# Down projection of a gated MLP in seven block products, taken in five stages of gate tiles

## The chip, the cores and the metric

One core of a Trainium2 chip runs the whole layer in one launch. The metric is the device time of that launch in microseconds (us). The kernel before takes 1263.61 us, the median of three runs (1263.59 to 1263.95).

## The reference

The layer takes 512 tokens of one group and 256 of another (768 in all), D_MODEL 1024. A token mixer comes first; the change doesn't touch it. What matters is the second sub-layer, a gated MLP with 2816 hidden channels (22 tiles of 128):

```python
def conv_ffn(hn, w_ffn_in, conv_w, conv_b, w_ffn_down):
    u, v = jnp.split(hn @ w_ffn_in, 2, axis=-1)
    up = jnp.pad(u, ((0, 0), (1, 1), (0, 0)))
    uc = conv_b
    for t in range(3):
        uc = uc + up[:, t:t + L] * conv_w[t]
    return (jax.nn.gelu(uc) * v) @ w_ffn_down

h = h + conv_ffn(rmsnorm(h, norm_ffn), ...)
return rmsnorm(h, norm_final)
```

Everything is float32. The down projection is a (768 x 2816) by (2816 x 1024) product.

## The kernel before

A float32 product is made of three TensorE passes: each operand is split into a high part (a rounded copy, ScalarE, `hi_...`) and a low part (the difference to it, VectorE, `lo_...`), and high x high, high x low and low x high are accumulated in PSUM. Weights come by DMA into two buffers (`raw`, `raw2`), and their two parts go into a ring of 8 places of 512 columns (`ring`). `PLACE` and `ORD` give each piece its place and its number; ScalarE and VectorE fill the ring some 5 or 6 places ahead of TensorE, in an order written out by hand (`hi_upto`, `lo_upto`), and semaphores (`flo`: low part written, `fdone`: product done) tie the engines.

The input projection already runs in seven block products for eight. Per pair i (one tile of u, one of v) there are seven products A11, A12, S2, S1, S3, A22, S4 of 4 x 3 matmuls with 384 token columns (line 1669). The weight blocks for S1, S2, S3 and A22 are differences, made by GpSimd (`combine`, lines 1362 to 1373). ScalarE and VectorE join the products (`first_copy`, `second_copy`, `third_copy`, `join_...`), then comes the convolution (`centre`, `conv`, line 1241), the GELU (line 730), the product with v (`gate`, line 1253) and the split of the result into `g` (`gate_hi` line 737, `gate_lo` line 1257).

The order is cut into three chunks, of 8, 8 and 6 pairs (`CHUNKS`). After the pairs of a chunk its part of the down projection runs (`down`, line 1730): for either half of the 1024 output columns, unit by unit of 256 channels, six token tiles of 128 x three passes, each a matmul of a 128x128 gate tile (stationary) with 512 weight columns (moving). Each token tile has a PSUM bank for a half; VectorE adds the finished bank to the stream `h` (`residual`, line 1137). In the last chunk the second half is taken token tile by token tile, so that the closing norm of one tile (square on ScalarE line 798, mean, root, scale, store) runs beside the matmuls of the next. The down weights are plain: one DMA of 512 KB per unit (line 393), one ScalarE copy (line 659) and one VectorE difference (line 1155) of 1024 columns, nothing for GpSimd.

At the end of a chunk A22 of the last pair waits for the copy of S3 out of its bank, since no other product can be put between:

```python
            def pair_end(i):
                pe.wait_ge(p13_cp, i + 1)
                product(i, A22, BANK_A[i % 2], False)
```

Of the kernel before, what the change touches and what calls it, by code (L numbers as in the profile page):

```python
# [30 lines left out]
ALU = mybir.AluOpType  # L31
ACT = mybir.ActivationFunctionType
F32 = mybir.dt.float32
# [21 lines left out]
CHUNKS = ((0, 8), (8, 16), (16, 22))  # L55
# [8 lines left out]
UNITS = U_D + NF  # L64
# [20 lines left out]
ORD, PLACE, UPLACE, FREED, PIECES = {}, {}, {}, {}, {}  # L85
# [3 lines left out]
for _lo, _hi in CHUNKS:  # L89
    for _f in taken(_lo, _hi):  # L90
        ORD[_f], PLACE[_f], PIECES[_p], FREED[_p] = len(ORD), _p, _f, (True, len(ORD) + 1)
        _p += 1
    for _n in range(U_D + _lo, U_D + _hi):
        UPLACE[_n] = _p
        PIECES[_p], PIECES[_p + 1] = None, _n
        FREED[_p] = FREED[_p + 1] = (False, _n + 1)
        _p += 2
# [4 lines left out]
def raw_of(i):  # L102

    return (i + (i >= CHUNKS[0][1])) % 2


def loads_of(i):
    return sum(raw_of(j) == raw_of(i) for j in range(i + 1))


REGION = 4 * (NT * D + 2 * 8 * T + 3072 + 4 * T + HALF + 14 * HK * HALF)
# [56 lines left out]
def build(nc, x_s, x_p, units, pairs, vec, w_final, ident_d, masks_d, rot_d, strips_d, y_s, y_p):  # L168
    with ExitStack() as ctx:
# [6 lines left out]
        def region(*tensors):  # L176
# [36 lines left out]
        _, g, raw2, tb, u2, v2, cb, mid, af = region(  # L213
            ("b0", [P, NT, D], F32), ("g", [P, 2, 8, T], F32R), ("raw2", [P, 2, UNIT], F32), ("tb", [P, 2, PIECE], F32),
            ("u2", [P, 2, T], F32), ("v2", [P, T], F32), ("cb", [P, T], F32), ("mid", [P, HALF], F32),
            ("af", [P, 7, 2, HK, HALF], F32R))
        *_, wfin, junk2, hw = region(
            ("c0", [P, NT * D + 2 * 8 * T + 3072 + 4 * T + HALF], F32), ("wfin", [P, D], F32), ("junk2", [P, PIECE], F32), ("hw", [P, NT, D], F32))

        _, sums0 = region(  # L220
            ("e0", [P, NT * D + 2 * 8 * T + 3072 + 4 * T + HALF], F32), ("sums0", [P, 7, 2, HK, HALF], F32))
# [28 lines left out]
        pu_ld = [sem("pair_u_loaded0"), sem("pair_u_loaded1")]  # L250
        pv_ld = [sem("pair_v_loaded0"), sem("pair_v_loaded1")]
# [4 lines left out]
        dn, out_rdy, out_rdy0 = sem("down_done"), sem("out_ready"), sem("out_first_half_ready")  # L256
        half_sq, half_var, root_done, weighed = sem("half_squares"), sem("half_variance"), sem("root_inverted"), sem("out_weighed")

        raws = (raw, raw2)

        def source(i, x):

            r = raws[raw_of(i)]
            if i == 0 and x in FIRST:
                return FIRST[x]
            return {A11: r[:, 0, 0:PIECE], A12: r[:, 0, PIECE:UNIT], S4: r[:, 1, PIECE:UNIT], S3: r[:, 1, 0:PIECE],
                    S1: tb[:, 0, :], S2: tb[:, 1, :], A22: tb[:, 1, :]}[x]
# [16 lines left out]
        BANK_A, BANK_C = (0, 6), 7  # L284

# [42 lines left out]
        def _(sp):  # L328
# [47 lines left out]
            for lo, hi in CHUNKS:
                for i in range(lo, hi):
                    if i == 1:

                        sp.wait_ge(w_done, 2 * NT)  # L380
                        sp.dma_start(raw2[:, 0, :], pairs[i, 0]).then_inc(pu_ld[1], 16)
                        sp.dma_start(raw2[:, 1, :], pairs[i, 1]).then_inc(pv_ld[1], 16)
                    elif i == 0 or i == lo + 1:
                        load_pair(i, None, U_D + lo - 1)
                    else:
                        load_pair(i, i - 2, None)
                last_raw = hi - 1 if raw_of(hi - 1) == 0 else hi - 2
# [19 lines left out]
        def _(act):  # L407
# [235 lines left out]
            def hi_piece(i, x):  # L643
                if x in (A11, A12):
                    act.wait_ge(pu_ld[raw_of(i)], 16 * loads_of(i))
                elif x == S4:
                    act.wait_ge(pv_ld[raw_of(i)], 16 * loads_of(i))
                else:
                    act.wait_ge(t_done, 4 * i + ((S1, S2, S3, A22) if i == 1 else (S1, S3, S2, A22)).index(x) + 1)
# [3 lines left out]

            def hi_unit(n):
                act.wait_ge(raw_ld[n % 2], 8 * (n - n % 2) + 16)
                p = UPLACE[n]
                await_place(act, p)
                await_place(act, p + 1)
                act.activation(ring[:, p % 8:p % 8 + 2, 0, :], pieces(raw[:, n % 2, :]), ACT.Copy).then_inc(hi_split, 1)
# [3 lines left out]
            def hi_upto(p):  # L663
                for q in range(hi_next[0], min(p, PLACES - 1) + 1):
                    if isinstance(PIECES[q], tuple):
                        hi_piece(*PIECES[q])
                    elif PIECES[q] is not None:
                        hi_unit(PIECES[q])
# [47 lines left out]
            def centre(i):  # L716
# [3 lines left out]
                if i >= 1:  # L720
                    act.wait_ge(g_lo, i)
# [10 lines left out]
            def gate_hi(i, lo):  # L732
                act.wait_ge(g32_done, i + 1)
                if lo > 0:

                    act.wait_ge(unit_done, U_D + lo)
                act.activation(g[:, 0, i - lo, :], cb[:], ACT.Copy).then_inc(g_hi, 1)
# [24 lines left out]
            for lo, hi in CHUNKS:  # L762
                for i in range(lo, hi):
# [18 lines left out]
                    if i > lo:  # L782
                        gate_hi(i - 1, lo)
                hi_upto(PLACE[hi - 1, A22] + 6)
                centre(hi - 1)
                gelu(hi - 1)
                gate_hi(hi - 1, lo)
                for n in range(U_D + lo, U_D + hi):
                    hi_upto(UPLACE[n] + 6)
            for t in range(NT):  # L790
                act.wait_ge(h_up, (1 + 2 * len(CHUNKS)) * NT - NT + t + 1)
                act.wait_ge(fdone, len(ORD))
                act.drain()
                act.activation(junk2[:], h[:, t, 0:PIECE], ACT.Square, accum_out=stat[:, 4, t:t + 1]).then_inc(half_sq, 1)
            for t in range(NT):
                act.wait_ge(h_up, (2 + 2 * len(CHUNKS)) * NT - NT + t + 1)
                act.drain()
                act.activation(junk2[:], h[:, t, PIECE:D], ACT.Square, accum_out=stat[:, 0, t:t + 1]).then_inc(sq_done, 1)
                act.wait_ge(var_done, 2 * NT + t + 1)
                act.activation(stat[:, 2, t:t + 1], stat[:, 1, t:t + 1], ACT.Sqrt).then_inc(sd_done, 1)  # L800
                act.wait_ge(root_done, t + 1)
                act.wait_ge(weighed, t + 1)
                act.activation(hw[:, t, 0:PIECE], hw[:, t, 0:PIECE], ACT.Copy, scale=stat[:, 3, t:t + 1]).then_inc(out_rdy0, 1)
# [3 lines left out]
        def _(dve):  # L807
# [344 lines left out]
            def lo_unit(n):  # L1152
                dve.wait_ge(hi_split, n + 1)
                p = UPLACE[n] % 8
                dve.tensor_tensor(ring[:, p:p + 2, 1, :], pieces(raw[:, n % 2, :]), ring[:, p:p + 2, 0, :].bitcast(F32),
                                  ALU.subtract).then_inc(lo_split, 1)

            def combine_second(x):

                r = raws[raw_of(1)]  # L1160
                b11, b12, b22 = r[:, 0, 0:PIECE], r[:, 1, 0:PIECE], r[:, 1, PIECE:UNIT]
                if x == S1:
                    dve.wait_ge(pu_ld[raw_of(1)], 16)
                    dve.wait_ge(pv_ld[raw_of(1)], 16)
                    dve.wait_ge(t_done, 4)
                    ins = dve.tensor_tensor(tb[:, 0, :], b12, b11, ALU.subtract)
                elif x == S3:
                    ins = dve.tensor_tensor(b12, b22, b12, ALU.subtract)
                else:
                    dve.wait_ge(t_done, 5)  # L1170
                    ins = dve.tensor_tensor(tb[:, 1, :], b22, tb[:, 0, :], ALU.subtract)
                ins.then_inc(t_done, 1)

            lo_next = [BASE]

            def lo_upto(p):
                for q in range(lo_next[0], min(p, PLACES - 1) + 1):
                    what = PIECES[q]
                    if isinstance(what, tuple):
                        i, x = what  # L1180
                        lo_piece(i, x)
                    elif what is not None:
                        lo_unit(what)
# [65 lines left out]
            def gate(i):  # L1249
                dve.wait_ge(gelu_done, i + 1)  # L1250
                dve.wait_ge(c12_dn, i + 1)
                dve.wait_ge(c22_dn, i + 1)
# [600 lines left out]
```

## Time and profile before

| | |
|---|---|
| median of 3 runs | 1263.61 us |
| profiled execution, its own time | 1264.54 us |
| span of its trace | 1262.7 us |
| TensorE (PE) busy | 1232.3 us, 98% |
| VectorE (DVE) busy | 711.9 us, 56% |
| ScalarE (ACT) busy | 490.9 us, 39% |
| GpSimd (POOL) busy | 128.9 us, 10% |
| down projection, matmuls | 792 |
| input projection of the MLP, matmuls | 1848 |

Times in the trace are counted from the start of the span. The duration of a matmul there contains its way through the pipeline, so the rate is to be read from a run of matmuls, not from one. Idle time stands in square brackets, with what ended it. The MLP runs from 738 us to the end.

### The profile page before, as it was taken

The page shows a single profiled execution, that of the slowest core. Times are in us where ns is not written, and L with a number is a line of the kernel's source. Part 1 is how long each engine was busy: PE and PEld are TensorE (multiplying, and loading weights), DVE is VectorE, ACT ScalarE, POOL GpSimd, SP SyncE. Part 2 cuts the span into 40 slices and gives each one's busy share as a digit, 9 for nine tenths or more (in the row PEclk, how much of TensorE's full clock was granted, in tenths as well). Part 3 has the DMA queues.
Part 4 walks back from the last instruction along what each step waited for, and adds up shares of the span by engine and source line. Part 5 has one row for each costly group of instructions (what it writes and reads, how often), then busy time and mean ns, then how long its engine had stood idle before and what let it go on. Part 6 is the DMA issues. An engine that isn't in the chain of part 4 may idle for free.

```text
span 1262.7 us, 18036 instructions
## 1 busy us (share of the span) xinstructions
PE 1232.3 (98%) x7088; PEld 1120.7 (89%) x7088; DVE 711.9 (56%) x969; ACT 490.9 (39%) x724; POOL 128.9 (10%) x93
## 2 busy tenths in 40 slices
PE   6999999999999999999999988999999999999998
PEld 5999899989998998888888878998889998899986
DVE  7494586377368463223223698775237774337755
ACT  5353344245146152212221255554125653135534
POOL 0000000000000000000000303430124420124200
PEclk9999999999999999999999999999999999999999
DMA  4311111101121112121215102222201213112122
GB/s 171 136 35 51 63 51 51 62 33 50 34 78 36 46 37 68 67 67 50 76 56 184 34 34 86 82 68 78 89 34 67 67 42 121 72 34 81 53 84 100
DMA packets 23180, 86.10 MB, mean 68 GB/s; under 512 B 2512, under 2 KB 2768, under 8 KB 23120
## 3 DMA queue, kind: packets, MB, share of 16 engines
q1 hardware_dynamic: 22544, 83.90, 19.4%
q10 hardware_dynamic: 576, 1.38, 0.3%
q8 instruction: 41, 0.67, 0.2%
q14 instruction: 19, 0.16, 0.0%
HBM read 82.12 MB, written 3.15 MB: 68 GB/s over the span
## 4 chain that ended last, share of the span: by engine, by line
PE 92%; DVE 4%; DMA 1%; issue 1%; ACT 1%; DVEq 1%; SPq 0%; ACTq 0%
PE ps L1425 58%; PE ps L1669 23%; PE ps L1522 3%; PE ps L1462 3%; PE ps L1515 1%; PE ps L1532 1%; PE ps L1450 1%; DVE af L1196 1%; PE ps L1452 1%; DVE h L1137 1%; DMA raw<-in_units 1%; DVE ring L1150 1%; PE ps L1407 0%; PE ps L1498 0%; PE ps L1507 0%
## 5 line engine op out<-in xcount | busy, mean ns | idle before, releaser
L1425 PE MATMUL ps<-hn,ring 128*128 128x256 f32 (+1 forms) x2544 | 462.5, 337 | 0.3 <-DVE hn L839 0.3
L1425 PEld LDWEIGHTS ps<-hn,ring 128*128 128x128 f32 x2544 | 388.3, 191 | 46.7 <-issue 0.7
L1669 PE MATMUL ps<-af,ring 128*128 128x384 f32 x1848 | 325.7, 336 | 10.9 <-DVE af L1196 3.9
L1669 PEld LDWEIGHTS ps<-af,ring 128*128 128x128 f32 x1848 | 321.3, 189 | 15.0 <-DVE af L1196 4.8
L1425 PE MATMUL ps<-ring,g 128*128 128x512 f32 x792 | 180.9, 390 | 0.8 <-issue 0.8
L1425 PEld LDWEIGHTS ps<-ring,g 128*128 128x128 f32 x792 | 148.4, 188 | 32.6 <-issue 2.0
L810 DVE TENSOR_TENSOR ring<-raw,ring 128x1024 fp32r<-128x1024 f32 x68 | 83.1, 1224 | 119.2 <-ACT ring L415 114.8
L464 ACT ACTIVATE sig<-ps 128x768 f32<-128x768 f32 x36 | 29.2, 812 | 179.9 <-PE ps L1425 179.8
L1150 DVE TENSOR_TENSOR ring<-raw,ring 128x512 fp32r<-128x512 f32 x88 | 74.0, 877 | 15.9 <-ACT ring L652 15.7
L415 ACT ACTIVATE ring<-raw 128x1024 fp32r<-128x1024 f32 x68 | 71.7, 1055 | 28.8 <-PE ps L1425 10.2
L1384 POOL TENSOR_TENSOR sums<-raw 128x512 f32<-128x512 f32 x1 | 1.3, 1289 | 706.9 <-DMA raw<-in_pairs 706.9
L1425 PE MATMUL ps<-gated,ring 128*128 128x512 f32 (+1 forms) x384 | 68.2, 337 | 0.0
L1425 PE MATMUL ps<-ring,merged 128*128 128x512 f32 x288 | 66.9, 391 | 0.1
L1425 PEld LDWEIGHTS ps<-gated,ring 128*128 128x128 f32 x384 | 59.6, 190 | 7.8
L888 DVE TENSOR_TENSOR pt<-ps,strips 128x512 f32<-128x512 f32 (+1 forms) x48 | 28.5, 601 | 65.3 <-PE ps L1452 65.3
L1425 PEld LDWEIGHTS ps<-ring,merged 128*128 128x128 f32 x288 | 53.6, 188 | 11.5 <-issue 0.5
L652 ACT ACTIVATE ring<-raw 128x512 fp32r<-128x512 f32 x88 | 52.3, 624 | 29.1 <-PE ps L1425 29.1
L1137 DVE TENSOR_TENSOR h<-ps,h 128x512 f32<-128x512 f32 x48 | 32.8, 691 | 42.4 <-PE ps L1425 42.2
L477 ACT ACTIVATE yc<-tree_k 128x768 f32<-128x768 f32 x28 | 25.6, 916 | 76.5 <-DVE tree_k L975 41.5
L1150 DVE TENSOR_TENSOR ring<-tb,ring 128x512 fp32r<-128x512 f32 x63 | 43.5, 694 | 16.5 <-ACT ring L652 16.5
L1241 DVE SCALAR_TENSOR_TENSOR cb<-u,vecs,cb 128x511 f32<-128x511 f32 x88 | 51.1, 622 | 2.0 <-issue 0.4
L652 ACT ACTIVATE ring<-tb 128x512 fp32r<-128x512 f32 x63 | 37.1, 621 | 32.3 <-PEq L1763 14.1
(158 smaller groups left out, 1210.5 us busy)
## 6 DMA issues: line engine op xcount, KB each, us to landing
raw<-in_units SPq DMA_DIRECT2D x90, 512.0 KB, 3.5
raw<-in_pairs SPq DMA_DIRECT2D x44, 512.0 KB, 3.4
strips<-in_strips SPq DMA_DIRECT2D x4, 896.0 KB, 4.5
x_in<-in_x_s SPq DMA_DIRECT2D x4, 512.0 KB, 5.5
h<-in_x_s SPq DMA_DIRECT2D x1, 2048.0 KB, 8.4
y_s<-hw SPq DMA_DIRECT2D x4, 512.0 KB, 2.6
x_in<-in_x_p SPq DMA_DIRECT2D x2, 512.0 KB, 7.5
h<-in_x_p SPq DMA_DIRECT2D x1, 1024.0 KB, 10.5
```

The source lines that it names most:

```text
L415: act.activation(ring[:, 2 * slot:2 * slot + 2, 0, :], pieces(raw[:, slot % 2, :]), ACT.Copy).then_inc(hi_split, 1)
L464: ins = act.activation(sig[:, u % 2, :], dense(u), ACT.Sigmoid)
L652: act.activation(place_of(i, x, 0), source(i, x), ACT.Copy).then_inc(fhi, 1)
L810: dve.tensor_tensor(ring[:, 2 * slot:2 * slot + 2, 1, :], pieces(raw[:, slot % 2, :]), ring[:, 2 * slot:2 * slot + 2, 0, :].bitcast(F32), ...
L888: dve.tensor_tensor(pt[:, (i % 4) * NS:(i % 4) * NS + width], ps[:, 4 + i % 2, 0:width], strips[:, a, c0:c0 + width], ALU.mult).then_inc(r ...
L1137: return dve.tensor_tensor(hs, ps[:, bank, :], hs, ALU.add).then_inc(h_up, 1)
L1150: dve.tensor_tensor(place_of(i, x, 1), source(i, x), place_of(i, x, 0).bitcast(F32), ALU.subtract).then_inc(flo, 1)
L1241: ins = dve.scalar_tensor_tensor(out=cs, in0=u2[:, i % 2, c0 + frm:c0 + frm + w - 1], scalar=vecs[:, V_CONV + tap * NF + i:V_CONV + tap * ...
L1425: ins = pe.matmul(out, w if stationary_w else x, x if stationary_w else w, start=start and i == 0, stop=stop and i == 2)
L1462: ins = pe.matmul(ps[:, 6 + m // 4, col:col + 64], pt[:, (i % 4) * NS + c * P:(i % 4) * NS + (c + 1) * P], rv[:, m * P + 64 * a:m * P + 64 ...
L1522: ins = pe.matmul(out(c * P, P), yc[:, c * P:(c + 1) * P], facing(tree_q[:], what, c * P, P), start=True, stop=True)
L1669: ins = pe.matmul(ps[:, bank, 0:HALF], ring[:, p, a, k * P:(k + 1) * P], af[:, x, b, k, :], start=first and k == 0 and j == 0, stop=k == H ...
```

## The change

The down projection too is made of seven block products. The token tiles are halved (0 to 2, 3 to 5), the output columns are halved, and the inner dimension is halved inside each pair q of gate tiles (tiles 2q and 2q+1). Per pair q there are seven products of 3 token tiles x 3 passes, each matmul in the shape of before (128x128 gate form stationary, 512 weight columns moving). The code below is its core:

```diff
-CHUNKS = ((0, 8), (8, 16), (16, 22))
+STAGES = ((0, 5, (0, 1)), (5, 9, (2, 3)), (9, 13, (4, 5)), (13, 17, (6, 7)), (17, 22, (8, 9, 10)))
+DOWN = [(A11, A12, S2, S1, S3, S4, A22)] * 4 + [(A11, A12, S2, S1, S4, S3, A22)]
+DEST = {A11: (0, 0), A12: (0, 0), S2: (0, 1), S1: (1, 1), S3: (1, 1), S4: (0, 1), A22: (1, 0)}
+ON_A = (A11, S2, S3, A22)
+            def down(hi, qs, d):
+                for n, x in enumerate(order):
+                    steps = [(q, t) for t in range(3) for q in qs]
+                    for q, t in steps:
+                        if t == 0:
+                            pe.wait_ge(flo, ORD[down_pair(q), x] + 1)
+                            pe.wait_ge(g_lo, gate_form(q, x))
+                        if q == q0:
...
+                            elif x in (S2, S1, S3, S4, A22):
+                                before = {S2: A11, S1: A12, S3: S2, S4: S1, A22: S3}[x]
+                                pe.wait_ge(h_up, base + 3 * order.index(before) + t + 1)
+                        for j, (a, b) in enumerate(((0, 0), (0, 1), (1, 0))):
+                            ins = pe.matmul(ps[:, down_bank(hi, x, t), :], gate_place(q, x, b)[:, t * P:(t + 1) * P],
+                                            ring[:, p, a, :], start=q == q0 and j == 0 and x in (A11, A12, S1), ...)
```

Stage by stage: pairs 0 to 4 of the input projection, then q = 0, 1; pairs 5 to 8, then q = 2, 3; and so on; pairs 17 to 21, then q = 8, 9, 10. Partial sums of A11, S2, S3, A22 pile up in one set of banks, those of A12, S1, S4 in another, and after each product VectorE adds the three banks as they then stand to the quarter of `h` that `DEST` names (`down_sums`). The last product runs token tile by token tile into the closing norm; tiles 0 to 2 are finished after S4.

The down weights are loaded as pairs of half-columns, and are treated as the pairs of the input projection: seven pieces of 512 columns per q for ScalarE and VectorE, four differences of 512 columns for GpSimd. S1 is now written over the first raw block, so that it waits for the low part of A11:

```diff
+            if x == S1:
+                eng.wait_ge(pu_ld[raw_of(j)], 16 * loads_of(j))
+                eng.wait_ge(pv_ld[raw_of(j)], 16 * loads_of(j))
+                eng.wait_ge(flo, ORD[j, A11] + 1)
+                ins = eng.tensor_tensor(b11, b12, b11, ALU.subtract)
```

The gate tiles have forms too. The even tile gives A11 (its first 384 tokens) at once; with the odd tile VectorE makes four sums of 384 columns, and six forms are split:

```diff
             def gate(i):
+                if i % 2 == 0:
+                    dve.tensor_tensor(ge[:], cb[:], v2[:], ALU.mult).then_inc(g32_done, 1)
+                    return
                 dve.tensor_tensor(cb[:], cb[:], v2[:], ALU.mult).then_inc(g32_done, 1)
+                dve.tensor_tensor(GATE[S3], ge[:, 0:HALF], ge[:, HALF:T], ALU.subtract).then_inc(gs_done, 1)
...
+                dve.tensor_tensor(GATE[S2], GATE[A22], GATE[S3], ALU.subtract).then_inc(gs_done, 1)
+                dve.tensor_tensor(GATE[S1], ge[:, HALF:T], GATE[A22], ALU.add).then_inc(gs_done, 1)
+                if i == NF - 1:
+                    gate_lo(i - 1)
...
+                dve.tensor_tensor(GATE[S4], GATE[A12], GATE[S2], ALU.subtract).then_inc(gs_done, 1)
+            def gate_lo(i):
+                for x in GATES[:1] if i % 2 == 0 else GATES[1:]:
+                    dve.wait_ge(g_hi, gate_form(q, x))
+                    dve.tensor_tensor(gate_place(q, x, 1), GATE[x], gate_place(q, x, 0).bitcast(F32), ALU.subtract)
```

In the first four stages the forms of a q are finished one pair before the stage ends. In the last one q = 10 needs tiles 20 and 21; its raw weights (`raw3`) and its forms (`gf3`) lie in the memory of the token forms `af` of the input projection, so ScalarE's `gate_hi` for it waits for the last product of pair 21. The `pe.drain()` at the end of each half of a chunk is gone. The order of the work in the input projection is as before but for the stage borders.

## Rows read from the trace of the kernel before

**Rows 1.** The page, busy time of each engine over the span.
```profile
PE 1232.3 (98%) x7088; PEld 1120.7 (89%) x7088; DVE 711.9 (56%) x969; ACT 490.9 (39%) x724; POOL 128.9 (10%) x93
```

**Rows 2.** Chain that ended last from 1050 us: shares by line; pieces as start, us, what.
```profile
by line: PE ps L1425 52.3%; PE ps L1669 39.5%; DVE h L1137 1.9%; DMA raw<-in_units 1.7%; issue 1.1%; ACT junk L798 0.3%; ACT hw L803 0.3%; DVE ring L1150 0.3%; ACT v L714 0.2%; ACT mid L707 0.2%; DVE stat L1343 0.1%; ACT stat L800 0.1%; DVE
...
1052.18 32.68 PE ps L1425 x144
```

**Rows 3.** TensorE in order of time: start, us, instructions, idle before and its releaser.
```profile
1085.12 32.91 PE L1425 MATMUL ps<-ring,g 128*128 128x512 f32 x144 [0.26 <-issue]
1118.29 81.36 PE L1669 MATMUL ps<-af,ring 128*128 128x384 f32 x468 [0.26 <-DVE h L1137]
1199.83 2.36 PE L1669 MATMUL ps<-af,ring 128*128 128x384 f32 x12 [0.17 <-ACT mid L707]
1202.77 4.43 PE L1669 MATMUL ps<-af,ring 128*128 128x384 f32 x24 [0.58 <-ACT v L714]
1207.04 24.68 PE L1425 MATMUL ps<-ring,g 128*128 128x512 f32 x108
1231.98 24.75 PE L1425 MATMUL ps<-ring,g 128*128 128x512 f32 x108 [0.26 <-issue]
```

**Rows 4.** Busy time by stretch: window, its length, PE, PEld, DVE, ACT, POOL, clock, DMA.
```profile
867.80:934.08 66.28, 65.76 (x289) 53.83 (x289) 22.23 (x29) 11.41 (x15) 8.85 (x6) 1.00 0.20 70
934.08:1052.00 117.92, 117.12 (x672) 116.48 (x673) 81.01 (x120) 63.87 (x114) 37.27 (x26) 1.00 0.20 68
1052.02:1118.29 66.27, 65.75 (x290) 53.83 (x289) 22.77 (x29) 11.42 (x15) 8.88 (x6) 1.00 0.21 71
```

**Rows 5.** VectorE groups by shape from 740 us: count, busy us, mean ns, idle before.
```profile
L1150 DVE TENSOR_TENSOR ring<-tb,ring 128x512 fp32r<-128x512 f32 x63 | 43.5, 694 | 16.5 <-ACT ring L652 16.5
L1137 DVE TENSOR_TENSOR h<-ps,h 128x512 f32<-128x512 f32 x36 | 24.6, 692 | 34.0 <-PE ps L1425 33.9
L1257 DVE TENSOR_TENSOR g<-cb,g 128x768 fp32r<-128x768 f32 x22 | 21.1, 959 | 4.7 <-ACT g L737 2.7
L1233 DVE TENSOR_TENSOR v<-ps,v 128x384 f32<-128x384 f32 x22 | 12.3, 558 | 31.1 <-ACT v L714 31.1
```

**Rows 6.** VectorE in order of time, within two neighbouring pairs.
```profile
955.85 1.28 DVE L1150 TENSOR_TENSOR ring<-raw,ring 128x512 fp32r<-128x512 f32 x2
962.08 2.38 DVE L1150 TENSOR_TENSOR ring<-raw,ring 128x512 fp32r<-128x512 f32 x2
965.58 0.56 DVE L1221 TENSOR_TENSOR u<-ps,u 128x384 f32<-128x384 f32 x1 [1.12 <-PE ps L1669]
```

**Rows 7.** GpSimd in order of time, beside the second of these.
```profile
962.34 1.58 POOL L1362 TENSOR_TENSOR tb<-raw 128x512 f32<-128x512 f32 x1 [2.30 <-DVE ring L1150]
963.99 1.63 POOL L1365 TENSOR_TENSOR raw<-raw 128x512 f32<-128x512 f32 x1
```

**Rows 8.** VectorE from the last product of the last pair (TensorE 1207.2).
```profile
1207.71 2.36 DVE L1241 SCALAR_TENSOR_TENSOR cb<-u,vecs,cb 128x511 f32<-128x511 f32 x4
1210.98 0.96 DVE L1253 TENSOR_TENSOR cb<-cb,v 128x768 f32<-128x768 f32 x1 [0.91 <-ACT cb L730]
```

**Rows 9.** The start of the MLP: VectorE, then TensorE, in order of time.
```profile
763.91 3.47 DVE L1150 TENSOR_TENSOR ring<-raw,ring 128x512 fp32r<-128x512 f32 x2
769.45 3.20 DVE L1241 SCALAR_TENSOR_TENSOR cb<-u,vecs,cb 128x511 f32<-128x511 f32 x4
...
769.58 12.59 PE L1669 MATMUL ps<-af,ring 128*128 128x384 f32 x62 [2.88 <-DVE v L1227]
```

**Rows 10.** Busy time by stretch at the start of the MLP (columns as Rows 4).
```profile
760.00:770.00 10.00, 5.67 (x31) 5.03 (x30) 9.96 (x13) 5.81 (x11) 5.47 (x4) 1.00 0.13 50
770.00:780.00 10.00, 10.00 (x51) 10.00 (x50) 8.93 (x13) 6.26 (x11) 3.17 (x3) 0.83 0.31 107
```

**Rows 11.** The closing norm, VectorE and ScalarE in order of time.
```profile
1244.53 0.69 DVE L1137 TENSOR_TENSOR h<-ps,h 128x512 f32<-128x512 f32 x1 [1.37 <-PE ps L1425]
1246.75 0.49 DVE L1348 TENSOR_SCALAR hw<-hw,stat 128x512 f32<-128x512 f32 x1
1256.76 0.69 DVE L1137 TENSOR_TENSOR h<-ps,h 128x512 f32<-128x512 f32 x1 [1.15 <-PE ps L1425]
1258.98 0.72 ACT L803 ACTIVATE hw<-hw,stat 128x512 f32<-128x512 f32 x1 [0.23 <-DVE stat L1346]
```

**Rows 12.** DMA issues: source, KB each, median us from issue to landing.
```profile
raw<-in_pairs SPq DMA_DIRECT2D x44, 512.0 KB, 3.4
```

More of the change, by code:

```diff
@@ L795, in _ @@
[L795 to L799, printed above, removed]
+                if hi == NF:
+                    gate_hi(NF - 2)
+                    gate_hi(NF - 1)
+                for n, x in enumerate(DOWN[d]):
+                    hi_upto(PLACE[down_pair(qs[-1]), x] + 6)
+                    if n == 1 and hi < NF:
+                        gate_hi(hi - 1)
+                    if hi == NF and n == 2:
+                        act.wait_ge(fdone, ORD[NF - 1, S4] + 1)
+                        for t in range(3):
+                            act.wait_ge(h_up, down_base(d) + 3 + t + 1)
+                            squares(t, early(t), stat[:, 4, t:t + 1]).then_inc(half_sq, 1)
@@ new lines, in _ @@
+            base, order = down_base(len(STAGES) - 1), DOWN[-1]
+            for t in range(3):
+                act.wait_ge(h_up, base + 3 * order.index(S4) + t + 1)
+                squares(t, late(t), stat[:, 0, t:t + 1]).then_inc(sq_done, 1)
+            act.wait_ge(var_done, 2 * NT + 1)
+            act.activation(stat[:, 2, 0:3], stat[:, 1, 0:3], ACT.Sqrt).then_inc(sd_done, 1)
+            act.wait_ge(root_done, 1)
+            act.wait_ge(weighed, 3)
+            for t in range(3):
+                act.activation(hw[:, t, early(t)], hw[:, t, early(t)], ACT.Copy, scale=stat[:, 3, t:t + 1]).then_inc(out_rdy0, 1)
@@ L1249, in gate @@
             def gate(i):
+                q = i // 2
                 dve.wait_ge(gelu_done, i + 1)
@@ L1329, in _ @@
[L1329 to L1338 removed]
+                if hi == NF:
+                    gate(NF - 1)
+                    gate_lo(NF - 1)
@@ L1393, in _ @@
                 combine_tokens(pool, 0, x, s_done, 0)
-            combine(1, A22)
-            for i in range(2, NF):
-                for x in (S1, S3, S2, A22):
-                    combine(i, x)
+            pool.wait_ge(t_done, DIFF[1, S3])
+            for j, x in DIFFS[7:]:
+                difference(pool, j, x)
         @blk.tensor
@@ L1784, in _tables @@
+            for d, (lo, hi, qs) in enumerate(STAGES):
+                ffn(lo, hi, d)
+                down(hi, qs, d)
 def _tables():
@@ L1821, in _units @@
     out += [rows(w_out, k, half) for half in range(2) for k in range(KD // 2)]
-    for f0, f1 in CHUNKS:
-        out += [rows(w_ffn_down, k, half) for half in range(2) for k in range(f0 // 2, f1 // 2)]
     assert len(out) == UNITS
     pairs = [np.stack([cols(w_ffn_in, f * P), cols(w_ffn_in, FF + f * P)]) for f in range(NF)]
+    pairs += [np.stack([rows(w_ffn_down, q, 0), rows(w_ffn_down, q, 1)]) for q in range(NQ)]
     return np.stack(out), np.stack(pairs)
```

425 lines of the change are left out of this document (205 added, 220 removed).

## The prediction

> **What bounds the kernel now.** I read the page's busy shares first: TensorE is busy 98% of the span, and no other engine is over 56% [rows 1]. The chain of waits says the same for the part that the change touches: from 1050 us on 92% of it is TensorE's matmuls [rows 2]. So the time is the number of matmuls by their rate, plus the few gaps. The timeline of TensorE gives both: the three down parts are unbroken runs, the only gaps being 0.26 us after each drain, about 0.2 us once at a chunk's end, and 0.58 us where A22 of a chunk's last pair waits for the copy of S3 [rows 3]. The clock is at its upper level (2.4 GHz, granted 1.00) in these stretches [rows 4].
>
> **Matmuls removed.** Before there are 22 units x 2 x 6 tiles x 3 passes = 792, after 11 x 7 products x 3 tiles x 3 passes = 693. The shape stays, so the rate is the present one: 32.68 us / 144 = 0.227 us [rows 2]. After: 693 x 0.227 = 157.3 us. Before, the three down parts took 66.28 and 66.27 us [rows 4], and 1207.04 to 1256.73, 49.7 us [rows 3]: 182.2 us, drains and restarts included. Difference: **-24.9 us** (of it 22.5 by the count alone, the rest the five drains that go, each 0.26 us of idle and a pipeline run-out).
>
> **Two more stage ends.** The input projection keeps its 1848 matmuls. The wait for the copy of S3 now comes five times, not three: 0.58 us idle and some 0.16 us of run-out, twice: **+1.5 us** [rows 3].
>
> **VectorE in the down parts.** Here lies most of the work that is added. It was busy 22 of 66 us there [rows 4], a wide cover. Two pieces of 512 columns issue in 1.28 us [rows 6], and a sum out of PSUM takes 0.69 us [rows 5]. In a stage of two q a product lasts 18 x 0.227 = 4.09 us of TensorE; VectorE has 2 pieces (1.28), 3 sums (2.07) and a drain (0.1) in it: 3.45 us, 84%. Each product starts on banks whose sums of two products ago must be done, tile by tile, so VectorE may lag about one product. At a stage's start it does lag: in the pair before, the odd gate tile adds 4 sums and 6 low parts of 384 columns (0.47 us issue to issue, from the 0.56 us of a 384-column operation [rows 5]) for one low part of 768: (4 + 6) x 0.47 - 0.87 = +3.8 us. Following its order by hand, with the last convolution ending 4.6 us after the stage's last input product (2.9 us now [rows 8]), two pieces and the sums of A11 end at 7.9, gate and A12's sums at 12.2, S2's first sum at 14.7; S3 wants that one at 4 x 4.09 = 16.4 us. Slack 1.7 us. GpSimd's eight differences per stage eat some of it. In the trace two of them (1.58 and 1.63 us) made two pieces of VectorE take 2.38 us where they take 1.28 [rows 6, 7], and at 764 us two pieces took 3.47 us, at 769 us a convolution 3.20 for 2.36 [rows 8, 9]: 0.55 to 0.9 us lost per difference that overlaps. Two or three fall before S3. Bounds 0 and 2 us a stage; I take 0.3, as VectorE gains 0.6 us on TensorE in each product: **+1.2 us** for four stages. The Trainium skill ("SBUF — State Buffer", section "SBUF: two separate sides") has a rule that speaks against the change: a VectorE operation with both inputs in SBUF and a GpSimd operation exclude each other for the whole instruction. The rows above agree in kind, not in size: were each of three differences to cost a full 1.6 us, a stage would lose 3 x 1.6 - 1.7 = 3.1 us, four 12.4, and the sum below would be +2.2 us; I count that case in rival B. Sums out of PSUM have one input in SBUF and would be free by the rule.
>
> **VectorE in the input projection.** 81.0 us busy in 117.9 [rows 4], 10.0 us of 14.56 per pair. Two pairs gain 4 sums (1.9 us) and 7 low parts for 2 (+1.6): 23.5 us of 29.1. The odd one alone reaches 14 us, and the join after it, for which it now sits idle 1.12 us [rows 6], comes about 2 us late. Who waits: S1 of the next pair, two products (4.1 us) after it, for `join_last`. I take 0; bounds 0 and 0.5 us in each of ten odd pairs.
>
> **Weights.** The 22 unit loads become 22 half-pair loads of the same 512 KB; each lands in 3.4 us [rows 12]. At a down part's end the next pair's first load waits for the low part of A22 of q0, which is only two places ahead of it; 3.4 + copy 0.6 + low part 0.7 = 4.7 us against 4.1 us for two places. VectorE, blocked on it, loses about 1 us of a lead of 5 places (10 us). ScalarE was held longer by such a load at each of the present chunk ends, which cost TensorE 0.17 us [rows 3]. I take 0; the bound upwards is that VectorE's 1 us passes on to TensorE at each of nine borders.
>
> **The start of the last stage.** This is the one gap I expect plainly. TensorE takes the first tile of q 8, 9 and 10 at once, and for q 10 the A11 form of tile 20 must be ready after 6 x 0.227 = 1.36 us. Its low part is written by `gate_lo(20)`, which stands behind `gate(21)` and three sums in VectorE's queue, and that behind the last convolution and GELU. Now the gate product of the last pair starts at 1210.98, 3.8 us after the last input product [rows 8]. Then: 0.95 (product), 3 sums with one semaphore between (1.5), the low part (0.5), a semaphore: 6.8 us. Gap 6.8 - 1.4 = 5.4 us. Before, the gate tiles of the last pair were wanted only at the end of a half, so the same chain was hidden; that cover is gone. At the same time GpSimd makes the nine differences S1, S2, S3 of three q, 1.3 to 1.6 us each without a pause; four or five fall on this chain: 4.5 x 0.55 to 0.9 = 2.5 to 4 us. I take 3.0: **+8.4 us** (bounds 5.4 and 10).
>
> **The clock.** Before 770 us TensorE was busy 5.7 of 10 us, the last gap 2.88 us, and the granted clock then fell to 1.2 GHz for a while (mean 0.83 in the next 10 us) [rows 9, 10]; 62 matmuls of 384 columns took 12.59 us [rows 9], where at the rate of 468 in 81.36 us [rows 3] they take 10.8. A gap of over 5 us should do the same: **+1.8 us** (bounds 0 and 3.5).
>
> **The end.** The last product gives a token tile every 9 x 0.227 = 2.04 us, where now it is 4.09. The closing chain of one tile, from the sum (1244.53) to the end of the scaling (1247.24), is 2.71 us and had 1.37 us to spare [rows 11]. Now it is the slower one. Besides, VectorE comes late to it: in the last stage, from S1 on, it has the pieces, the sums, nine weighings and three scalings. By hand, from S2's end: sums of S1 end at 7.0, of S4 13.0, weighing and scaling of tiles 0 to 2 at 17.1, sums of S3 19.9 (TensorE 18.4), weighings 22.2; then three chains of 2.71 us, the third starting at 27.6, when TensorE ended at 24.7. From the last sum on the end is as now. **+3.0 us** (bounds 1.3, the chains alone, and 4.5).
>
> **Sum.** -24.9 + 1.5 + 1.2 + 8.4 + 1.8 + 3.0 = -9.0 us. The profiled execution took 1264.54 us, so 1255.5; it lies 0.9 us above the median of the runs, which gives **1254.6 us**.
>
> **Rivals.** *A, the gap is small:* GpSimd's differences are done early or don't meet the chain, and the clock holds: -24.9 + 1.5 + 5.4 + 3.0 = -15.0, 1248.6 us. For it: GpSimd is busy only 10% [rows 1]. Against: the nine differences start just there. *B, VectorE becomes the bound (slower):* if each of GpSimd's differences costs it 0.9 us, a product in a two-q stage needs 3.45 + 8 x 0.9 / 7 = 4.5 us, more than TensorE's 4.09; x 28 products = +11 us, and the odd pairs, at 14 us of 14.56, give 0.5 each, +5: -9.0 - 1.2 + 11 + 5 = +5.8, 1269.4 us. It decides from 0.56 us per difference on; the rows straddle that, but sums out of PSUM, 60% of the work, showed no stretching (692 ns mean [rows 5]), and VectorE's idle time takes up part. *C, between:* lateness in the stages of 1 us each, ten small waits in odd pairs (3 us): -9.0 + 2.8 + 3 = -3.2, 1260.4 us. *D, the weights come late:* 1 us at nine borders: 1263.6 us, no change. That the change doesn't remove the matmuls it says is excluded: they are counted in the loops.
>
> **How the numbers follow.** Forecast 0.50, A 0.20, C 0.16, D 0.05, B 0.09. The range leaves out B, D, and the lower part of A: 1249.5 to 1262 us. This kernel can be told from no change at about 0.2%, 2.5 us: faster 0.50 + 0.20 + 0.16 and a little of D, 0.88; within 0.2% 0.04; slower 0.08.
>
> **What would show it.** 693 matmuls in the down parts at 0.227 us each; a gap of 7 to 9 us on TensorE right after the first 6 of the last part, released by VectorE's low part of a gate form, and a granted clock under 1.00 behind it; five gaps of 0.6 us released by the copy of S3; VectorE busy 80 to 100% in the down parts, with pieces stretched and sums not; the last tiles' sums 2.7 us apart. The forecast is wrong if TensorE pauses inside the two-q parts (B, C), if the last gap is under 5 us (A), or if waits for DMA stand at the borders (D).

## The result, and the profile after

The changed kernel takes 1286.37 us, the median of four runs (1284.81 to 1288.06), against 1263.6 us before: ratio 1.018, interval 1.0163 to 1.0198. I had forecast 1254.6 us: the change costs 22.8 us where 9 were to be gained. The span of the profiled execution is 1283.9 us, 21.2 us more than before. The page after, busy shares (answers to [rows 1]):

```profile
PE 1222.6 (95%) x6989; PEld 1111.4 (87%) x6989; DVE 872.8 (68%) x1189; ACT 528.7 (41%) x832; POOL 195.7 (15%) x137
```

TensorE has its 99 matmuls less and is busy 9.7 us less, but it now stands idle. Where, its timeline shows (columns as [rows 3]; L1750 is the input projection, L1833 the down projection):

```profile
818.67 2.35 PE L1750 MATMUL ps<-af,ring 128*128 128x384 f32 x12 [0.58 <-ACT v L765]
826.28 3.71 PE L1750 MATMUL ps<-af,ring 128*128 128x384 f32 x12 [5.26 <-DVE v L1288]
829.83 28.76 PE L1833 MATMUL ps<-ring,gf 128*128 128x512 f32 x126
...
921.34 3.95 PE L1750 MATMUL ps<-af,ring 128*128 128x384 f32 x12 [5.26 <-DVE v L1288]
...
1014.29 4.21 PE L1750 MATMUL ps<-af,ring 128*128 128x384 f32 x12 [3.12 <-DVE v L1288]
...
1111.05 4.21 PE L1750 MATMUL ps<-af,ring 128*128 128x384 f32 x12 [5.23 <-DVE v L1288]
...
1217.11 6.02 PE L1750 MATMUL ps<-af,ring 128*128 128x384 f32 x24 [3.57 <-ACT v L765]
1222.97 1.55 PE L1833 MATMUL ps<-ring,gf 128*128 128x512 f32 x6
1231.33 37.58 PE L1833 MATMUL ps<-ring,gf 128*128 128x512 f32 x156 [6.81 <-DVE gf L1331]
```

The gap is at the end of each of the first four stages, before S4 of the last pair, and it is ended by VectorE's `join_third` (L1288). The 12 matmuls behind it take 3.7 to 4.2 us, not 2.35: the granted clock (1.00 is 2.4 GHz, 0.50 is 1.2 GHz) has a mean of 0.59, 0.55, 0.50 and 0.50 over these four stretches. In the fifth stage the gap stands one product earlier, before A22, and is ended by ScalarE's copy of S3. Set against the kernel before, from the starts in these timelines:

| part | before | after | difference | forecast |
|---|---|---|---|---|
| input projection of the MLP | 336.3 | 368.2 | +31.9 | +1.5 |
| down parts | 182.2 | 169.1 | -13.1 | -13.5 |
| from the last matmul to the end | 6.0 | 8.4 | +2.4 | +3.0 |

(The five input parts after are 738.25 to 829.83, 858.62 to 925.13, 953.78 to 1018.29, 1048.38 to 1115.06 and 1144.09 to 1222.97; the last matmul ends at 1275.5.) So the whole error is in the first line: gaps of 5.26 + 5.26 + 3.12 + 5.23 + 3.57 = 22.4 us, slow matmuls behind them 6.7 us in four stages and 1.6 in the fifth, and one wait of 0.58 us more for the copy of S3 (four of them, for three before; the fifth is the 3.57 us). Against my terms the four `join_third` gaps and their slow matmuls are 25.6 us of the error, and the fifth stage's end 4.6 us.

What VectorE did before the second of these gaps, and GpSimd beside it:

```profile
909.69 1.28 DVE L1232 TENSOR_TENSOR ring<-raw,ring 128x512 fp32r<-128x512 f32 x2
910.89 2.05 DVE L1315 TENSOR_TENSOR cb<-cb,v 128x768 f32<-128x768 f32 x1
912.87 1.62 DVE L1316 TENSOR_TENSOR gs<-ge 128x384 f32<-128x384 f32 x1
914.60 1.47 DVE L1319 TENSOR_TENSOR gs<-cb,gs 128x384 f32<-128x384 f32 x1
915.99 1.62 DVE L1320 TENSOR_TENSOR ge<-ge,cb 128x384 f32<-128x384 f32 x1
917.53 1.62 DVE L1325 TENSOR_TENSOR ge<-cb,gs 128x384 f32<-128x384 f32 x1
919.07 1.75 DVE L1232 TENSOR_TENSOR ring<-raw,ring 128x512 fp32r<-128x512 f32 x1
920.74 0.55 DVE L1288 TENSOR_TENSOR v<-ps,v 128x384 f32<-128x384 f32 x1
```

```profile
910.54 1.59 POOL L327 TENSOR_TENSOR raw<-raw 128x512 f32<-128x512 f32 x1 [8.77 <-DVE ring L1232]
912.21 1.87 POOL L332 TENSOR_TENSOR tb<-raw 128x512 f32<-128x512 f32 x1
914.04 1.61 POOL L327 TENSOR_TENSOR raw<-raw 128x512 f32<-128x512 f32 x1
915.73 1.46 POOL L332 TENSOR_TENSOR tb<-raw 128x512 f32<-128x512 f32 x1
917.15 3.12 POOL L335 TENSOR_TENSOR raw<-raw 128x512 f32<-128x512 f32 x2
```

GpSimd's S1, S2 and S3 of both q run without a pause from 910.54 to 920.27, and six VectorE operations with both inputs in SBUF alternate with them one for one. An operation of 384 columns takes up to 1.62 us where it takes 0.55 alone. (I wrote above that the forms of a q are finished one pair before a stage ends. Here they are made in the time of the last pair itself: the four sums from 912.87, the six low parts from 921.21 to 924.10, beside S4.)

### The profile page after: what moved, and what is told of

Its sections match the earlier page's. It is cut to its first block, busy times and chain, and to the rows that moved or that the text cites. A ratio compares the mean times of both kernels' runs of the same rounds, so it can differ in the third digit from the quotient of the medians.

```text
span 1283.9 us, 18435 instructions
## 1 busy us (share of the span) xinstructions
PE 1222.6 (95%) x6989; PEld 1111.4 (87%) x6989; DVE 872.8 (68%) x1189; ACT 528.7 (41%) x832; POOL 195.7 (15%) x137
## 4 chain that ended last, share of the span: by engine, by line
PE 82%; DVE 10%; issue 2%; ACT 2%; DVEq 2%; DMA 1%; POOL 0%; SPq 0%; ACTq 0%; POOLq 0%
PE ps L1507 43%; PE ps L1750 18%; PE ps L1833 9%; PE ps L1604 3%; PE ps L1544 3%; DVE ring L1232 2%; PE ps L1597 1%; PE ps L1614 1%; DVE gf L1331 1%; PE ps L1532 1%; DVE cb L1296 1%; DMA raw<-in_pairs 1%; DVE af L1251 1%; DVE cb L1315 1%; PE ps L1534 1%
## 5 line engine op out<-in xcount | busy, mean ns | idle before, releaser
L1750 PE MATMUL ps<-af,ring 128*128 128x384 f32 x1848 | 335.6, 342 | 33.2 <-DVE v L1288 18.9
L1750 PEld LDWEIGHTS ps<-af,ring 128*128 128x128 f32 x1848 | 327.2, 192 | 40.9 <-DVE v L1288 20.1
L1833 PE MATMUL ps<-ring,gf 128*128 128x512 f32 x693 | 162.0, 396 | 7.0 <-DVE gf L1331 6.8
L1833 PEld LDWEIGHTS ps<-ring,gf 128*128 128x128 f32 x693 | 132.8, 192 | 35.3 <-issue 7.8
L1232 DVE TENSOR_TENSOR ring<-raw,ring 128x512 fp32r<-128x512 f32 x164 | 128.2, 814 | 15.6 <-ACT ring L713 15.3
L713 ACT ACTIVATE ring<-raw 128x512 fp32r<-128x512 f32 x164 | 96.5, 621 | 57.3 <-DMA raw<-in_pairs 44.6
L1219 DVE TENSOR_TENSOR h<-ps,h 128x512 f32<-128x512 f32 x117 | 75.0, 686 | 18.1 <-PE ps L1507 8.1
L327 POOL TENSOR_TENSOR raw<-raw 128x512 f32<-128x512 f32 x31 | 45.2, 1459 | 171.9 <-DVE ring L1232 171.9
L1296 DVE SCALAR_TENSOR_TENSOR cb<-u,vecs,cb 128x511 f32<-128x511 f32 x88 | 65.1, 780 | 1.9
L339 POOL TENSOR_TENSOR tb<-raw,tb 128x512 f32<-128x512 f32 x32 | 42.3, 1324 | 157.1 <-DVE ring L1232 157.1
L1232 DVE TENSOR_TENSOR ring<-tb,ring 128x512 fp32r<-128x512 f32 x64 | 58.8, 921 | 1.4 <-ACT ring L713 0.6
## 6 DMA issues: line engine op xcount, KB each, us to landing
h<-in_x_p SPq DMA_DIRECT2D x1, 1024.0 KB, 10.7
```

The source lines that it names most:

```text
L327: ins = eng.tensor_tensor(b11, b12, b11, ALU.subtract)
L339: ins = eng.tensor_tensor(second, b21, second, ALU.subtract)
L713: act.activation(place_of(i, x, 0), source(i, x), ACT.Copy).then_inc(fhi, 1)
L1219: return dve.tensor_tensor(hs, ps[:, bank, :], hs, ALU.add).then_inc(h_up, 1)
L1232: dve.tensor_tensor(place_of(i, x, 1), source(i, x), place_of(i, x, 0).bitcast(F32), ALU.subtract).then_inc(flo, 1)
L1296: ins = dve.scalar_tensor_tensor(out=cs, in0=u2[:, i % 2, c0 + frm:c0 + frm + w - 1], scalar=vecs[:, V_CONV + tap * NF + i:V_CONV + tap * ...
```

## The experiments

**e1: the join ahead of the sums** (order of VectorE, stage ends only).

```diff
+                    ahead = i == hi - 1 and i % 2 == 0
                     if i > lo:
-                        gate(i - 1)
+                        gate(i - 1, not ahead)
+                    if ahead:
+                        join_third(i)
+                        gate_sums(i - 1)
                     lo_upto(PLACE[i, S3] + 5)
-                    if i > 0:
+                    if i > 0 and not ahead:
                         join_third(i)
```

In the last pair of a stage (`ahead`) `gate` makes the product with v alone, and `gate_sums` the four sums.

> Only VectorE's order at the ends of the first four stages is changed: join_third of the last pair comes right behind the product with v, ahead of the four gate sums and one weight piece. Theory T (the sums and GpSimd's six differences for the coming down part meet in VectorE's queue ahead of join_third, and the product S4 of the last pair waits for it): the product with v ends at 912.9 us, the copy of S3 at 913.7, so the join ends near 914.3, before A22 ends at 916.1: the four gaps of 5.3, 5.3, 3.1 and 5.2 us go, and so do the slow matmuls right behind them (12 in 3.7 to 4.2 us for 2.35). About 24 us less, some of it given back as later work in the down parts: 1260 to 1266 us. Theory R (the late raw weights hold ScalarE, and through it everything): ScalarE's order is untouched, so the gaps stay and the time is 1284 to 1288 us.

1287.61 us (ratio 1.019, 1.0173 to 1.0207): nothing gained, where I had expected 1260 to 1266. The time falls in the range that I gave to theory R (1284 to 1288), but by R the gaps would have stayed where they were. TensorE's timeline in the second stage:

```profile
915.46 4.43 PE L1760 MATMUL ps<-af,ring 128*128 128x384 f32 x24 [0.58 <-ACT v L765]
919.73 4.96 PE L1843 MATMUL ps<-ring,gf 128*128 128x512 f32 x21
926.41 3.72 PE L1843 MATMUL ps<-ring,gf 128*128 128x512 f32 x15 [1.72 <-DVE ring L1232]
934.05 22.25 PE L1843 MATMUL ps<-ring,gf 128*128 128x512 f32 x90 [3.92 <-DVE h L1219]
```

The gap before S4 is gone, but 1.72 + 3.92 = 5.6 us of waits stand a few us later, before a weight piece and before the sums. So it is not the order: VectorE is behind by its whole work in this stretch, and the first who needs it pays. That the gap before S4 went also speaks against ScalarE and the loads as its cause.

**e2: the down differences cut to 8 columns** (q 0 to 9, `b11[:, 0:8]` and so on; the rest of these blocks is left uncombined).

> GpSimd's differences for the down weights of q 0 to 9 are 8 columns wide, not 512 (the weight blocks of these products stay uncombined beyond them: part of the computation is left out). VectorE's order and work are those of the changed kernel. Theory T: without GpSimd's reads the product with v, the sums and the piece ahead of join_third take 0.87 + 4 x 0.47 + 0.6 and some 0.5 us of waits, 3.9 us, not 9.9: join_third at 914.7, no gap left at the four stage ends, 1258 to 1264 us. Rival Q (VectorE's own added work is the delay, GpSimd only incidental): the gaps shrink by under a third and the time is over 1278 us. Rival R (raw weights late): gaps unchanged.

1254.48 us (0.9926, 0.991 to 0.9943), 32 us less than the changed kernel and 3.5 us under the range I gave; it measures a cost only, since it doesn't compute the layer. VectorE in the same stretch, same operations:

```profile
903.87 0.95 DVE L1317 TENSOR_TENSOR cb<-cb,v 128x768 f32<-128x768 f32 x1
904.74 0.55 DVE L1318 TENSOR_TENSOR gs<-ge 128x384 f32<-128x384 f32 x1
...
906.82 0.69 DVE L1234 TENSOR_TENSOR ring<-raw,ring 128x512 fp32r<-128x512 f32 x1
907.42 0.55 DVE L1290 TENSOR_TENSOR v<-ps,v 128x384 f32<-128x384 f32 x1
```

From the product with v to the join it takes 3.55 us, against 9.85 us above: six full differences cost 6.3 us, 1.05 us each. About 0.9 of the 6.3 us were spare (here the join ends at 907.97 us, and S4 follows A22 near 908.8); 5.4 are left for TensorE, and S4 starts 5.5 us late in the changed kernel. All four gaps are gone, and the down parts run 126 matmuls in 28.77 us. The last part's gap stays (5.56 us, before the form of q 10).

**e5: the kernel before, in five chunks** (`CHUNKS = ((0, 4), (4, 8), (8, 12), (12, 16), (16, 22))`).

> The kernel before with five chunks of 4, 4, 4, 4 and 6 pairs in place of three of 8, 8 and 6; the same work, two more borders. My prediction priced two more borders at 1.5 us and the drains of two more chunks at 4 x 0.42 us, so 1265 to 1267.5 us. Rival S (stage ends are dear by themselves, and the gaps of the changed kernel are what a short chunk costs): over 1272 us.

1268.63 us (1.0038, 1.0025 to 1.005): two borders more cost 4.9 us, 2.5 us each: a little above my 1265 to 1267.5, and far from the changed kernel's loss.

**e7: e1, and A11 of the last part pair by pair**: `steps = [(q, t) for q in qs for t in range(3)]`.

> The first of these kernels, and A11 of the last down part taken pair by pair (q 8, 9, 10, three token tiles each) instead of token tile by token tile. The last part's first gap (6.8 us, for the low part of q 10's A11 form) should shrink by the 12 matmuls that now come before it, 12 x 0.227 = 2.7 us, and the clock's fall behind it may go: 2.7 to 5 us less than the first kernel. If the gap had another cause than the form of q 10, nothing changes.

1283.87 us, 3.7 us less than e1. The gap shrank from 8.54 us (e1) to 4.75 us (I had expected 2.7 us less), still ended by the low part of a gate form: it is the wait the prediction named.

**e8: the down differences on VectorE itself** (`difference(dve, ...)` behind the low parts of A11 and S2, with a semaphore of their own).

> The 44 differences of the down weights move from GpSimd to VectorE's own queue (S1, S2, S3 of a q behind the low part of its A11, A22 behind that of S2). VectorE gets 0.6 us more work for each, 3.6 us ahead of the late join in each of the four stages, and loses GpSimd's reads. Theory T' (a GpSimd difference holds VectorE off for its whole length, 1.3 us, whenever VectorE reads twice from SBUF, so that six of them cost 6.0 us ahead of the join): VectorE comes out 2 to 2.5 us ahead per stage, the gaps of 5.3 us shrink to about 3: 1270 to 1280 us. Rival Q' (it is simply too much work for the stretch, whoever does it; the cost of overlap is the 0.55 to 0.9 us of my prediction): about 0 to 4 us slower than the changed kernel, 1286 to 1291 us.

1277.8 us (1.0116, 1.0099 to 1.0133), within the expectation of T' and 8.6 us less than the changed kernel, although VectorE does 44 operations more. A difference costs it 0.60 to 0.73 us when it makes it itself, 1.05 us when GpSimd does:

```profile
908.20 0.69 DVE L336 TENSOR_TENSOR raw<-raw 128x512 f32<-128x512 f32 x1
908.93 0.69 DVE L341 TENSOR_TENSOR tb<-raw 128x512 f32<-128x512 f32 x1
909.54 0.68 DVE L344 TENSOR_TENSOR raw<-raw 128x512 f32<-128x512 f32 x1
```

A gap of 3.64 us is left at each of the four ends, ended by ScalarE's copy of S3, which waits for the product with v behind these six.

**e9: stages that end on an odd tile**, so that no sums and low parts of a gate stand ahead of the down part (the odd tile's four sums come after the third down product, its low parts in the next stage); only the line of the stages is shown here. **e10**: e9 with e7's order in the last part.

```diff
-STAGES = ((0, 5, (0, 1)), (5, 9, (2, 3)), (9, 13, (4, 5)), (13, 17, (6, 7)), (17, 22, (8, 9, 10)))
+STAGES = ((0, 6, (0, 1)), (6, 10, (2, 3)), (10, 14, (4, 5)), (14, 18, (6, 7)), (18, 22, (8, 9, 10)))
```

> Stages of 6, 4, 4, 4 and 4 pairs in place of 5, 4, 4, 4 and 5, same q: the pair before the last of a stage is now an even gate tile, which costs VectorE one product and no sums or low parts; the odd tile's four sums come after the third down product, its six low parts at the next stage's first pair, where no convolution stands in the queue. 4 x 0.47 + 5 x 0.47 = 4.2 us less on VectorE ahead of the down part, GpSimd's differences as they are. Theory T' : the lag was 5.3 us, of which 6.0 by GpSimd; with 4.2 us of two-input work gone fewer operations meet it, so the gaps at the four ends go to 0 to 1 us and the clock holds: 1258 to 1266 us. If the lag is only carried over to the sums of the down part, as in the first experiment, 1275 us and more.

> The one before, and A11 of the last down part pair by pair. The pair e1, e7 gave 3.7 us for this; the same here: 1254 to 1262 us, which would be at or below the kernel before the change.

1271.5 us (1.0065) and 1268.73 us (1.0044, 1.0028 to 1.0061): the large gaps at the ends are gone. e9 gained 15 us on the changed kernel, not the 20 to 28 I expected, and e10 missed its range (1254 to 1262) too. The differences now meet the last convolution, and TensorE waits for the sums three or four times a stage, 0.4 to 1.25 us each; in e9 the last part's gap for the form of q 10 also grew, from 6.81 to 8.63 us (3.96 in e10).

**e11: GpSimd's S3 (and so A22) of a q held back until the convolution is done** (`eng.wait_ge(conv_done, hi)`); **e12**: the loads of q 10 issued ahead of those of q 9; **e13**: e12 with the short differences of e2.

> e10, with GpSimd's S3 differences of the down weights (and so the A22 ones behind them) held back until the last pair's convolution is done, in the last stage until q 10's first form is out; they are wanted only for the fifth product. In e10 the convolution took 4.71 us for 2.36 beside them, and TensorE then waited about 3.5 us a stage for VectorE's sums. Theory T' (a difference costs only if two-input work of VectorE stands beside it; the sums out of PSUM are free): the convolution takes 2.4 to 3 us, the waits fall to 1 us a stage, the last stage's 4 us gap by 1 us: 1258 to 1262 us. If only the number of differences counts and not where they fall: 1267 to 1270 us.

> The one before, and the two loads of q 10 issued ahead of those of q 9. In e10 four half loads were issued within 2 us at 1193 to 1195 us, ScalarE stood 2.6 and 3.5 us for them, and TensorE 3.12 us for its copy. Theory: that gap goes, with the slow clock behind it, 3 to 5 us less than e11. If the DMA is not what holds ScalarE there: no change.

> The one before with the differences of q 0 to 9 cut to 8 columns (the rest of these blocks is left uncombined: computation left out). What the down differences still cost in the best arrangement. By T' 1 to 4 us less than e12; if over 6 us, the moves have hidden little.

1264.26 us (1.0009, 1.0 to 1.0018), 1262.53 us (0.9993, 0.9984 to 1.0002) and 1251.81 us (0.9906). The convolution of the second stage's last pair in e10, with three differences beside it (GpSimd busy from 929.13 to 934.01), and in e12, with none:

```profile
930.24 4.71 DVE L1296 SCALAR_TENSOR_TENSOR cb<-u,vecs,cb 128x511 f32<-128x511 f32 x4
```

```profile
929.48 2.36 DVE L1300 SCALAR_TENSOR_TENSOR cb<-u,vecs,cb 128x511 f32<-128x511 f32 x4
```

As T' says, it matters beside what a difference falls. e11 came short of its range (4.5 us gained over e10, 7 to 11 expected); e12's load gap, 2.58 us in e11, went to 0.58, yet only 1.7 us were gained, since the next gap, for q 10's A11 form, grew from 2.83 to 4.31 us. e13 shows 10.7 us still paid to the differences, far over my 1 to 4, though less than the 31.9 of the changed kernel (e2). It can be split by the starts of the stages: 1.5 to 1.8 us in each of the first four, 3.6 in the last.

**e14: e12, with the sums of the fifth to the seventh down product each ahead of the weight pieces that stood before them** (in the two-q parts). In e12 TensorE waits there for VectorE's sums, which stand behind pieces whose raw weights are late (up to 952.13 us ScalarE waits 10.15 us for a load, and then VectorE 1.63 us for ScalarE's copy, ahead of sums that are ready):

```profile
954.42 4.36 PE L1847 MATMUL ps<-ring,gf 128*128 128x512 f32 x18 [0.56 <-DVE h L1223]
960.00 54.38 PE L1762 MATMUL ps<-af,ring 128*128 128x384 f32 x312 [1.22 <-DVE h L1223]
```

```diff
+                    if hi < NF and n >= 4:
+                        down_sums(d, hi, qs, x, range(3))
                     if hi < NF or n < 6:
                         lo_upto(PLACE[down_pair(qs[-1]), x] + 5)
                     if hi < NF:
-                        down_sums(d, hi, qs, x, range(3))
+                        if n < 4:
+                            down_sums(d, hi, qs, x, range(3))
...
```

> e12, with VectorE's sums of the fifth and sixth product of a two-q down part put ahead of the weight pieces that stood before them (the first pieces of the next stage, whose raw weights are late). In e12 TensorE waits 0.46 to 0.58 us before the last down product and 1.22 us before the next stage's first product, each with a run-out of 0.16 us or more, for these sums. If VectorE's order at the border is the cause, these go: 5 to 8 us less than e12 (1254.5 to 1257.5 us). If VectorE is simply full there, they stay or move to a wait for a piece: 1260 to 1263 us.

**1252.67 us, ratio 0.9919 (0.9905 to 0.9933): 10.5 us faster than the kernel before**, the best version here, and 9.9 us less than e12 where I had expected 5 to 8. In its second, third and fourth stage the only pause left is the 0.58 us for the copy of S3 (the first has one of 0.45 us for the sums too):

```profile
921.96 4.43 PE L1765 MATMUL ps<-af,ring 128*128 128x384 f32 x24 [0.58 <-ACT v L769]
926.23 29.12 PE L1850 MATMUL ps<-ring,gf 128*128 128x512 f32 x126
```

**e15: e14, and the A11 form of tile 20 split ahead of the last convolution.** GpSimd's S3 differences of the last stage, which waited for that form, now wait for the third of the last four sums instead.

> The one before, and in the last stage the A11 form of tile 20, ready since long, is split ahead of the last convolution and GELU, not behind the last product and three sums. The gap of 4.3 us and the slow clock behind it (15 matmuls in 5.85 us for 3.4) are then gone: 4.3 + 0.16 + 2.4, 5 to 8 us less than the one before, 1247 to 1252 us. If the next form of q 10 (A12, behind the product with v) then becomes the wait, only 2 to 4 us.

1254.23 us (0.9931, 0.9918 to 0.9945): no gain, a miss. The gap for the form went, and a longer one came for a weight piece (A12 of q 10), which stands behind the six other forms, these stretched by GpSimd's held-back S3 (two low parts in 3.17 us for 1.01; in e14 the same two take 3.20):

```profile
1206.17 30.96 PE L1851 MATMUL ps<-ring,gf 128*128 128x512 f32 x129 [7.98 <-DVE ring L1237]
```

```profile
1199.41 3.17 DVE L1340 TENSOR_TENSOR gf<-cb,gf 128x384 fp32r<-128x384 f32 x2
```

In e14 TensorE goes on behind the same piece at 1206.33 us, after gaps of 4.30 and 2.04 us; here at 1206.17. So the form was not the last thing that it waited for.

## Why the prediction was wrong

**What held.** The matmuls removed and their rate: 126 take 28.75 us, 0.228 us each. In the four two-q parts VectorE was busy 88 to 89%, and the 312 matmuls of the second, third and fourth input part run unbroken, so the odd pairs there cost nothing, as I had it. The down parts as a whole came to -13.1 us against the -13.5 of my terms (-24.9 + 1.2 + 8.4 + 1.8), which is closer than the terms are. The gap for q 10's A11 form was 6.81 us for the 8.4 expected: the right wait in the right place, as e7 and e15 confirm, but my 3.0 us in it for GpSimd measured 1.25. Six of the nine differences were out before TensorE's last input product ended, and of the chain only the convolution was stretched (3.61 us for 2.36); in e2 the gap is 1.25 us shorter. In the other direction, the third and fourth part took 1.4 and 0.3 us more than the first two (28.7 us), since the clock was still low at their start (granted 0.71 and 0.89 in the first 3.7 and 3.9 us); 0.3 of the 1.4 is a wait for the sums.

```profile
1221.08 4.67 POOL L335 TENSOR_TENSOR raw<-raw 128x512 f32<-128x512 f32 x3
1223.65 3.61 DVE L1296 SCALAR_TENSOR_TENSOR cb<-u,vecs,cb 128x511 f32<-128x511 f32 x4
```

The closing chains came 2.80 us apart for 2.71, as these ends of scalings show, and the end cost 2.4 us for 3.0:

```profile
1274.58 0.49 DVE L1454 TENSOR_SCALAR hw<-hw,stat 128x512 f32<-128x512 f32 x1
1277.38 0.49 DVE L1454 TENSOR_SCALAR hw<-hw,stat 128x512 f32<-128x512 f32 x1
```

**The step that failed** is the one on VectorE ahead of and in the down parts, with its "Two or three fall before S3. Bounds 0 and 2 us a stage; I take 0.3". Two things in it were wrong. *The count and the place:* I let the differences meet VectorE after the stage's last product. In the trace all six (S1, S2, S3 of both q) start as soon as the low part of q0's A11 is written, 910.5 us, and fall on the product with v, the four sums and a piece; behind these stands `join_third`, for which S4 of the last pair waits in TensorE's queue. I priced the odd gate's extra work there (+3.8 us) and carried it on into the down part, but never asked who waits for the join; the border stood in my sum only as the copy of S3, 0.58 us. *The size:* I took 0.55 to 0.9 us per difference; with two-input operations back to back it is 1.05 us (e2 against the changed kernel), six times over: 6.3 us, of which 0.9 were spare. One of my own rows held the higher price. Two pieces from 763.91 to 767.38 us took 3.47 us for 1.28 in the kernel before, and beside them GpSimd ran two operations and began a third:

```profile
763.53 1.60 POOL L1373 TENSOR_TENSOR tb<-raw,tb 128x512 f32<-128x512 f32 x1 [37.25 <-DVE ring L1150]
765.37 1.47 POOL L1362 TENSOR_TENSOR tb<-raw 128x512 f32<-128x512 f32 x1 [0.23 <-POOL tb L1373]
766.91 1.60 POOL L1365 TENSOR_TENSOR raw<-raw 128x512 f32<-128x512 f32 x1
```

Put on the first two, the 2.19 us lost are 1.1 us each; spread over three they are 0.7. Once TensorE had stood 3 to 5 us, the clock cost another 1.4 to 1.9 us a time, which I had counted only for the last stage.

A second term failed at the end of the fifth stage: **Weights**, which I took at 0. There ScalarE's copy of S3 stood behind two pieces whose raw weights came late, and TensorE lost 3.0 us more than the 0.58 and 1.6 us by the clock. In e12, where the loads of q 10 go first, the wait is 0.58 us; in e11, without that, 2.58.

```profile
1215.54 1.15 ACT L713 ACTIVATE ring<-raw 128x512 fp32r<-128x512 f32 x2 [3.67 <-DMA raw<-in_pairs]
```

The Trainium skill's rule ("SBUF — State Buffer", "SBUF: two separate sides"), that a VectorE operation with both inputs in SBUF and a GpSimd operation exclude each other for its whole length, is what these rows look like: one for one, 1.62 us for 0.55. I had weighed it and taken the smaller size. A difference cost VectorE 1.05 us, a little under the 1.29 us that GpSimd takes for one alone. Its other half, that an operation with one input elsewhere is free, holds as well: three sums out of PSUM take 1.89 us with GpSimd idle and with it busy (at 939.29 and 947.35, GpSimd from 947.43):

```profile
939.29 1.89 DVE L1219 TENSOR_TENSOR h<-ps,h 128x512 f32<-128x512 f32 x3
...
947.35 1.89 DVE L1219 TENSOR_TENSOR h<-ps,h 128x512 f32<-128x512 f32 x3
```

**The rivals.** B had the engine right (VectorE) and the threshold too ("from 0.56 us per difference on"; it is 1.05), but the price too low, 1269.4 us, and the place wrong: not spread over the products but in one stretch before each down part. It had 0.09 where the rows straddled its threshold. D was not seen in the four stages; a load did hold the fifth one's end (3.57 us). C and A were not near. That e2 lands within 0.2 us of my forecast, 1254.6, is partly luck: by the same three lines as above it has +4.0, -16.1 and +2.4 us for my +1.5, -13.5 and +3.0. Its input projection still has the late copy in the last stage (2.33 us, and the clock behind it), and its down parts have none of the lateness and less of the gap that I had counted.

**Still open.** e14 won 2.3 to 2.5 us in each of the first four stages of e12 and nothing in the last; its down parts take 29.12 us for the 28.76 of e13, so little is left to the differences there. The last stage, where e13 is 3.6 us shorter than e12 and e14, and its gaps (4.30 and 2.04 us in e14) weren't mended, and e14's order together with short differences wasn't run.

## What to carry to other kernels

Before pricing work on a second engine as hidden, list what the first engine does in the same microseconds and whether those operations take both inputs from SBUF; if so, add the lengths, don't overlap them, and compare with doing it on the first engine (here 0.6 to 0.7 us against 1.05). When an engine falls behind, moving one operation ahead only changes who waits (e1, e15): take work out of the stretch, or let the other engine's work fall beside sums out of PSUM. A change of order pays where the engine itself stands idle ahead of work that is ready (e14). And follow every delayed instruction to the wait in TensorE's queue that it feeds, also ahead of the part that the change rewrites.

## What the runs showed of the hardware

A VectorE operation of 384 columns with both inputs in SBUF took 0.55 us alone and 1.47 to 1.62 us between GpSimd's operations; GpSimd's own of 512 columns took 1.29 us alone and 1.46 to 1.87 us. Around gaps of 3.1 to 5.3 us the clock fell to 1.2 GHz (granted mean 0.50 to 0.59 over the 12 matmuls behind them, which took 3.7 to 4.2 us for 2.35). In e1, where the lost time was cut in two, it was 1.00 behind the gap of 1.72 us and 0.71 in the 5.95 us behind the one of 3.92.
